# Two quarters of each of the last 24 cached key pages queued by SyncE instead of GpSimd, in a one-core decoder-layer kernel

## The reference, cut to what matters

```python
q, k, v, u = project_in(xs, l, attn_norm, w_in, q_norm, k_norm)
k_past = cache_k[l][page_table].reshape(db, past_len, 2 * N_HEADS, HEAD_DIM)
v_past = cache_v[l][page_table].reshape(db, past_len, N_HEADS, 2 * HEAD_DIM)
k_all = jnp.concatenate([k_past.astype(k.dtype), k], axis=1)
v_all = jnp.concatenate([v_past.astype(v.dtype), v], axis=1)
o = diff_attn_core(q, k_all, v_all, q_pos, k_pos, lam)
c, cs = conformer_conv(u, state_conv[l], dw_w[l], dw_b[l], conv_ln_g[l], conv_ln_b[l])
xs = finish_layer(xs, o, c, l, attn_subln, w_out, mlp_norm, w_up, w_down)
```

## Time and profile before

| what | value |
|---|---|
| median of three runs | 1622.88 us |
| the profiled execution | 1632.08 us, its span 1630.4 us |
| busy: PE, DVE, ACT, POOL | 93%, 60%, 36%, 26% |
| the two free bodies | about 534 to 660 us of the span |

### The profile page before, as it was taken

How to read it: one execution, slowest core, us unless ns; L and a number is a source line. 1 busy time by engine, 2 the same in 40 slices (tenths; PEclk the granted TensorE clock), 3 DMA queues, 4 the chain that set the end, 5 groups by cost and what they waited for, 6 DMA issues and landing times.

```text
span 1630.4 us, 31305 instructions
## 1 busy us (share of the span) xinstructions
PE 1514.5 (93%) x11203; PEld 1348.6 (83%) x11203; DVE 975.2 (60%) x1469; ACT 593.8 (36%) x929; POOL 419.7 (26%) x656
## 2 busy tenths in 40 slices
PE   5999898797877868899999999999999999999998
PEld 5988766565654433599999999999999999999998
DVE  3689857998998775353645544455444554445444
ACT  4433312122222332443544433443334433344432
POOL 4597656765787653000000000000000000000000
PEclk9999998998997977799999999999999999999999
DMA  7746799999999776834555545555455545555444
GB/s 201 215 144 185 234 321 333 353 341 327 342 305 349 252 236 221 289 118 154 155 158 165 168 167 162 164 165 166 167 166 162 164 165 167 167 163 163 165 166 148
DMA packets 163845, 340.50 MB, mean 209 GB/s; under 512 B 33915, under 2 KB 33971, under 8 KB 163168
## 3 DMA queue, kind: packets, MB, share of 16 engines
q1 hardware_dynamic: 120592, 267.29, 51.1%
q0 software_dynamic: 43168, 72.15, 14.5%
HBM read 334.00 MB, written 5.96 MB: 209 GB/s over the span
## 4 chain that ended last, share of the span: by engine, by line
PE 72%; issue 10%; DVE 7%; DMA 5%; POOL 3%; POOLq 2%; ACT 1%; SPq 0%; ACTq 0%
PE acc L691 21%; PE acc L693 21%; PE acc L692 21%; DMA k_page<-in_cache_k 3%; PE aux L777 2%; DVE k_page L1536 2%; POOL k_page L579 1%; PE aux L842 1%; POOLq L574 1%; DVE w_lo L1454 1%; DMA raw<-in_w_in 1%; PE acc L945 1%; PE aux L801 1%; POOLq L579 1%; PE acc L965 1%
## 5 line engine op out<-in xcount | busy, mean ns | idle before, releaser
L1454 DVE TENSOR_TENSOR w_lo<-raw,w_hi 128x1024 fp32r<-128x1024 f32 x368 | 451.5, 1229 | 410.2 <-ACT w_hi L1124 409.3
L691 PE MATMUL acc<-a_hi,w_hi 128*128 128x288 f32 (+1 forms) x1920 | 591.8, 308 | 35.2 <-DVE w_lo L1454 26.4
L1124 ACT CAST w_hi<-raw 128x1024 fp32r<-128x1024 f32 x368 | 384.9, 1049 | 586.5 <-DMA raw<-in_w_down 255.4
L693 PE MATMUL acc<-a_hi,w_lo 128*128 128x288 f32 (+1 forms) x1920 | 578.4, 301 | 0.0
L692 PE MATMUL acc<-a_lo,w_hi 128*128 128x288 f32 (+1 forms) x1920 | 578.2, 301 | 0.0
L691 PEld LDWEIGHTS acc<-a_hi,w_hi 128*128 128x128 f32 x1920 | 367.6, 191 | 72.5 <-DVE w_lo L1454 36.5
L579 POOL DMA_DIRECT2D k_page<-in_cache_k x512 | 332.1, 649 | 204.5 <-issue 89.3
L692 PEld LDWEIGHTS acc<-a_lo,w_hi 128*128 128x128 f32 x1920 | 368.3, 192 | 0.5
L693 PEld LDWEIGHTS acc<-a_hi,w_lo 128*128 128x128 f32 x1920 | 368.4, 192 | 0.0
L693 PE MATMUL acc<-h_hi,w_lo 128*128 128x288 f32 x1024 | 302.2, 295 | 0.0
L692 PE MATMUL acc<-h_lo,w_hi 128*128 128x288 f32 x1024 | 301.5, 294 | 0.0
(11 more groups left out here) (224 smaller groups left out, 892.6 us busy)
## 6 DMA issues: line engine op xcount, KB each, us to landing
k_page<-in_cache_k POOLq DMA_DIRECT2D x512, 128.0 KB, 6.6
raw<-in_w_up SPq DMA_DIRECT2D x128, 512.0 KB, 3.7
raw<-in_w_down SPq DMA_DIRECT2D x128, 512.0 KB, 3.6
v_page<-in_cache_v SPq DMA_DIRECT2D x120, 512.0 KB, 7.6
raw<-in_w_in SPq DMA_DIRECT2D x80, 512.0 KB, 6.0
raw<-in_w_out SPq DMA_DIRECT2D x32, 512.0 KB, 3.7
k_page<-in_cache_v SPq DMA_DIRECT2D x8, 512.0 KB, 5.5
x_nat<-in_x_prompt SPq DMA_DIRECT2D x3, 1024.0 KB, 8.9
```

What stands on the lines that cost most here:

```text
L691: mm(out, wh, ah, start=(kt == 0), stop=False)
L693: last = mm(out, wl, ah, start=False, stop=(kt == KT - 1))
L1124: nc.scalar.copy(w_hi[:, j % RAW], raw[:, j % RAW]).then_inc(hi_ok, 1)
L1454: v.tensor_tensor(w_lo[:, j % RAW], raw[:, j % RAW], w_hi[:, j % RAW].bitcast(F32), ALU.subtract)\
```

## The change

SP gets a function `half_keys`, which queues quarters 1 and 3 of a key page on SP, counted by new semaphores `kh_in`; POOL's `load_keys` queues only quarters 0 and 2 of these pages (`whole=False`). This holds for the last 24 key pages, index 104 to 127: pages 8 to 15 of sequence 6 and all of sequence 7. DVE's turn of such a page waits for both semaphores, in one instruction as before. SP handles four pages at a time (`key_group`), at six places in its list of value loads:

| batch | key pages (sequence: pages) | waits for the end of | stands in SP's list just ahead of the load of values |
|---|---|---|---|
| 1 | 6: 8 to 11 | score(6, 0) | (5, 2) |
| 2 | 6: 12 to 15 | score(6, 1) | (5, 6) |
| 3 | 7: 0 to 3 | score(6, 2) | (5, 10) |
| 4 | 7: 4 to 7 | score(6, 3) | (5, 14) |
| 5 | 7: 8 to 11 | score(7, 0) | (6, 2) |
| 6 | 7: 12 to 15 | score(7, 1) | (6, 6) |

```diff
+SPLIT = N_PAGES * (PAIR_V + 1) + KS
...
+        kh_in = [sem(f"kh_in{r}") for r in range(KS)]
...
+            def half_keys(s, j):
+
+                r = sp.value_load(pages_sb[0:1, ds(N_PAGES * s + j, 1)], min_val=0, max_val=n_phys - 1)
+                sp.wait_ge(sc_mm, NG * s + j // SG - 1)
+                for b in (1, 3):
+                    sp.dma_start(key_quarter(j % KS, b), key_rows(r, b)).then_inc(kh_in[j % KS], 16)
+
+            def key_group(i):
+                if i % SG == 0 and SPLIT + i < N_PAGES * N_SEQ:
+                    for j in range(SPLIT + i, SPLIT + i + SG):
+                        half_keys(j // N_PAGES, j % N_PAGES)
...
                 for j in range(N_PAGES):
+                    if keys:
+                        keys(j)
...
-            with sp.Fori(PAIR_V, N_SEQ - 2) as s:
-                body(s)
+            body(PAIR_V, keys=key_group)
             for i in range(2, N_PAGES):
+                key_group(N_PAGES + i - 2)
                 load_values(N_SEQ - 2, i)
...
-                for b in (0, 2, 1, 3):
+                for b in (0, 2, 1, 3) if whole else (0, 2):
...
-                load_keys(PAIR_V + 1, j)
+                load_keys(PAIR_V + 1, j, whole=False)
...
-                    load_keys(s, j)
+                    load_keys(s, j, whole=False)
...
-                dve.wait_ge(k_in[p % KS], 64 * (p // KS + 1))
+                if p < SPLIT:
+                    dve.wait_ge(k_in[p % KS], 64 * (p // KS + 1))
+                else:
+                    n = (p - SPLIT) // KS + 1
+                    dve.wait_ge(k_in[p % KS], 64 * (SPLIT // KS) + 32 * n)
+                    dve.wait_ge(kh_in[p % KS], 32 * n)
```

More of the change, by code:

```diff
@@ L437, in _, with body @@
                 load_w(ATT_FIRST, j, w_src(ATT_FIRST, j))
-            def body(vs, n=None, nxt=None, last=False):
+            def body(vs, n=None, nxt=None, last=False, keys=None):
                 for j in range(N_PAGES):
+                    if keys:
+                        keys(j)
                     if j + 2 < N_PAGES:
@@ L570, in _, with load_keys @@
                 pool.dma_start(conv_sample[0, s, 0:TAPS - 1 - DEC, :], st[s, DEC:TAPS - 1, :]).then_inc(kc_out, 16)
-            def load_keys(s, j, used=True):
+            def load_keys(s, j, used=True, whole=True):
                 r = pool.value_load(pages_sb[0:1, ds(N_PAGES * s + j, 1)], min_val=0, max_val=n_phys - 1)
```

## The result

The changed kernel took 1649.65 us (median of four runs, 1643.21 to 1653.51) beside 1624.18 us of the kernel before (median of four, 1622.68 to 1639.64). The ratio, which is taken over the runs and not from the two medians, is **1.0132, 95% interval 1.0100 to 1.0165**: 21.4 us of 1624.18. The medians by themselves lie 25.5 us apart. The forecast was +2.0 us, its range ended at 1636. The profiled execution took 1653.51 us, its span 1651.9; against the span before that is 21.5 us.

What follows compares the result with a forecast made beforehand. PE was taken as 72% of the chain of waits, the free bodies not bound by POOL. Terms 0.6 + 2.6 + 0.5 - 1.7 = +2.0 us on 1622.88 gave 1624.9 us; own range 1621 to 1631, 8 in 10 within 1617 to 1636.

Steps and rivals of the forecast that it cites:

- The price of a batch: SP's list: four half pages at 1.09 + 0.47 = 1.56 us each, so the value load behind goes out 6.2 us late.
- the text's own upper price of 8.7 us for a batch: SP's time for four half pages if the second quarter costs 1.09 us; the low price was 5.7 us.
- the sum's ends: Bounds of the summed change of +2.0 us: 0.8 - 2.7 = -1.9 and 1.3 + 4.7 + 1.9 = +7.9 us.
- rival 2: PE from 640 to 660 us: the clock gives back 4.6 us; with 1.7 for keys, 1616.6 us; stretches can fall too; chance 0.12.
- SP is always at that wait in time: SP's waits for scores: the value load ahead of each batch waits for values PE takes before that score, so no delay.
- Batch 4 as the largest term: Behind score(6, 3): (5, 15) lands 2.4, 4.2 or 6.3 us late; after 1.6 already waited, +0.8, +2.6 or +4.7 us.
- Batches 2 and 6: Behind score(6, 1) and score(7, 1): (5, 6) late by 0 to 1.3 us, taken +0.6; (6, 6) by 0 to 1.9, +0.5.
- Batches 1, 3 and 5 at 0: Behind score(6, 0), score(6, 2), score(7, 0): (5, 2), (5, 10) and (6, 2) come in time, 0 us each.
- Keys' waits, -1.7: DVE in the free bodies: earlier keys remove the 1.7 us wait on the chain; bounds 0 and -2.7 us.
- Rival 1: SP's keys clog its queue, value pages land after 10.0 us, (5, 15) first: +14.9 us, 1638 us; chance 0.2.
- The test named in the text: Forecast wrong if DVE's turn of page 14 of sequence 7 comes no later than 102.2 us after score(6, 0); some 104 expected.
- The doubt about the eight engines: DMA landings: SP's 48 key quarters may share eight engines with value pages waiting behind; longest landings, sum +7.9 - 1.7 = +6.2 us.

Runs made afterwards that it cites:

- experiment 9: Changed kernel, but POOL queues all four quarters; SP only waits for each score and reads the page number five times per page: 1.0130 to the kernel before.
- experiment 1: Changed kernel with SP's key quarters in a plain shape, 32 rows of 4 KB (wrong rows of the page): 1.0071 to the kernel before.
- 8: Kernel before, but quarters 1 and 3 of the last 24 key pages are queued by nobody, POOL queueing the other two: 0.9991 to the kernel before.
- 12: Changed kernel, but SP queues only quarter 3 of each of the 24 pages and POOL three: 1.0151 to the kernel before.

## Why the prediction was wrong

**The step that failed is "The price of a batch"**: 6.2 us, where 12.15 were measured. It took a half page as a full page's spacing plus a second plain transfer, and those rows are DMAs with a simple shape on both sides. The key quarter's price on SP stood in no row. POOL's 0.65 us a quarter was the nearest row of that very transfer; with it a page comes to 0.76 + 2 x 0.65 = 2.06 us and a batch to 8.2, so it would not have reached 12.15 either. Two things were missing: the DMA itself (0.71 to 0.92 us instead of 0.33 to 0.47), and the page read behind it (0.77 us instead of 0.27, as in the reads between value loads). With them a page takes 3.01 us, and four make the batch. The range failed with it: the text's own upper price of 8.7 us for a batch was not carried into the sum's ends.

With 12.15 in place of 6.2, the text's own steps and median landings give +3.2 for (5, 2), +5.3 for (5, 6), 10.1 - 1.6 = +8.5 for (5, 15), +1.0 for (6, 2), +6.5 for (6, 6), less 1.7: **+22.8**. That this lies near the 21.4 measured is in part luck. PE's waits bear out two of the places: 3.78 us for (5, 6), and 8.88 for (5, 14) and (5, 15). But PE did not wait for (5, 2) or (6, 6) at all, and for (6, 2) and (6, 3) it waited 3.91 us. All its waits together grew by 16.1 us, where the late values of that sum make 24.5. The rest of the loss goes with the clock, which the sum put at nothing (rival 2 named it, as a gain, and said that it can fall as well). On record are 66 runs of the kernel before, at mean clocks of 0.970 to 0.953, in 1618.5 to 1636.7 us; seven of them, at 0.955 or 0.956, took 1631.2 to 1635.2. The changed kernel's run at 0.955 took 1647.09, so at an equal clock some 12 to 16 us are left. Its other runs were at 0.951, 0.951 and 0.960, those of experiment 9, with no key on SP, at 0.950 to 0.953. Whether PE's idle time brought the clock down, no run separates. So the mechanism, value loads that go out late by SP's time, is shown; the sum place by place is not.

- *"SP is always at that wait in time"*: wrong for batches 3 and 6. Batch 3's score ended at 570.03 and SP came to it at 575.39, batch 6's at 636.17 and 640.58, because the value loads behind the batch before were still going out. Such lateness follows from the price: with the cheap batch of experiment 1, SP was in time at all six.
- *Batch 4 as the largest term*: right in place. Forecast +2.6; batch 4 alone cost some 9 us. *Batches 2 and 6* were next in the forecast; with the even batches alone PE waited 6.19 and 4.08 us for them. In the changed kernel batch 2 cost 3.78 us of waiting and batch 6 none.
- *Batches 1, 3 and 5 at 0*: nearly. Odd batches alone cost 0.28%, and in the changed kernel PE waited 3.57 us for (6, 2), behind batch 5.
- *Keys' waits, -1.7*: DVE's wait did go, but the ceiling measured in 8 is zero within its interval.
- *Rival 1, value pages that land late*: its landings of 10 us and more did not come in the changed kernel (median 4.7 us for pages issued in 584 to 616; 7.0, at most 8.3, in 619 to 641), though its sign and place were right. Where POOL kept three quarters (12) they did come.
- *Rival 2, the clock*: the second body did run at a higher clock, and the stretch behind it at a lower one; the two stretches together came out 0.4 us longer, with 3.9 us of new waits among them. In the first body the clock took instead of giving (0.75 after 0.90).
- *The test named in the text*: DVE's turn of page 14 of sequence 7 was the second of two that began at 658.51, some 123 us after score(6, 0), where 104 was expected and 102.2 stood before.

**The doubt about the eight engines** looked in the wrong direction. The Trainium skill ("DMA: Bandwidth & Descriptors", on why a DMA increments its semaphore by 16) also states that on SP's path the issuing sequencer itself writes the part of the count that no engine posts. The nine increments agree with eight engines and one more write; by this the 8 outermost rows would bear on SP's own time, where 0.84 us a page were measured, more than on the landings, for which the rule was cited. The same page ("Issuing engines are not separate DMA queues") says that starting DMAs on several engines at once saves only the time that the sequencer takes to start them, "which is usually small relative to the DMA itself". For one transfer that agrees here: 0.78 us of SP's time, and a value page's landing of 4.7. For a batch it does not: eight transfers with their reads took 12.15 us, and what stood behind them waited for all of it. The Trainium skill ("Perfetto Trace Analysis", on the hardware path's DMA instruction) states that such a row shows the making of descriptors and not the movement of data; the trace agrees: a value load's row on SP is 0.33 us long (L421), and the landing in the chain above took 4.40 us.

## What to carry to other kernels

Before a transfer is moved to another queue, price its issue by the shape of both its sides, and count it for everything behind it on that queue: a transfer that is off the path on one engine stands ahead of one that is on the path on the next. Where no row shows that shape on that engine, the price is open: here neither a plain transfer nor the same transfer on the other engine gave the price of a batch, and the range has to say so. And ask first what the relief can bring at its best: a kernel with the work simply left out tells it in one experiment.

## What the runs showed that was not expected

- Reading a page's number costs SP 0.27 us between value loads and 0.77 us behind a key quarter with 8 outermost rows. Behind one with 16, itself dear at 0.61 us, it is 0.27 again: the long read goes with the quarters that count nine increments, not with the price of the transfer.
- Dealing the rows of a key page out 16 or 32 at a time, with the same bytes in the same runs of 1 KB, made the kernel before 5.1 and 5.3% slower, and the median landing of its value pages over the whole kernel went from 7.6 us (first row, rows by 8) to 15.1 (by 16) and 15.3 (by 32):

```profile
DMA to landing us min/median/max: 3.4/7.6/13.8
```
```profile
DMA to landing us min/median/max: 3.5/15.1/23.3
```
```profile
DMA to landing us min/median/max: 3.4/15.3/22.1
```

All quarters are POOL's in these three kernels, and they differ in nothing but the order of the rows. Why that order holds up the value pages was not tested.
